# Rotary key by tokens, rotary queries from two half blocks, seven PSUM banks in the first FFN and wider mixer margins in a Hymba-style layer

## The reference

```
h = h + 0.5 * swiglu(rmsnorm(h, g_ffn1), w_gate, w_up, w_down)      # D_FF = 2816
u = rmsnorm(h, g_mix); proj = u @ w_in                              # 1184 columns
c_q (256) | c_kv (128) + k_pe (32) | q_s (512) | k_s (128) | v_s (128) = split(proj)
# latent attention, 8 heads, causal over the whole sequence
q = rmsnorm(c_q) @ w_q_b  -> per head 64 plain + 32 rotary
k_pe = rope(k_pe, cos, sin)                                         # one rotary key for all heads
kv = rmsnorm(c_kv) @ w_kv_b -> per head 64 key + 64 value
s = (q_nope . k_nope + q_pe . k_pe) * 96**-0.5; o_mla = softmax(s) @ v
# local attention, 8 query heads, 2 key heads, window 128, sinks, T5 bias -> o_swa
h = h + concat(rmsnorm(o_mla), rmsnorm(o_swa)) @ w_o
h = h + 0.5 * swiglu(rmsnorm(h, g_ffn2), ...)
out = rmsnorm(h, g_final)

def rope(x, cos, sin):            # x1, x2: the two halves of the last axis (16 + 16)
    return concatenate([x1 * cos - x2 * sin, x2 * cos + x1 * sin])
```

## Time and profile before

| | |
|---|---|
| median of 3 runs | 4984.26 us (4982.69 to 4986.34) |
| profiled execution | 4978.47 us |
| its span (core 2, the slowest) | 4976.9 us |
| spans of the 8 cores | 4958.9 to 4976.9 us |
| TensorE busy | 97% of the span |
| VectorE, ScalarE busy | 56%, 38% |
| GpSimd busy | 2% |

### The profile page before, as it was taken

How to read it: one execution, slowest core, us unless ns; L and a number is a source line. 1 busy time by engine, 2 the same in 40 slices (tenths; PEclk the granted TensorE clock), 3 DMA queues, 4 the chain that set the end, 5 groups by cost and what they waited for, 6 DMA issues and landing times.

```text
span 4976.9 us, 93066 instructions; the slowest of 8 cores (4958.9 to 4976.9 us)
## 1 busy us (share of the span) xinstructions
PE 4827.9 (97%) x29209; PEld 2350.5 (47%) x29784; DVE 2795.0 (56%) x6313; ACT 1895.0 (38%) x3567; POOL 91.2 (2%) x154
## 2 busy tenths in 40 slices
PE   7899999999999999999999999999999999999998
PEld 3344444445444444544544444454544444445444
DVE  4366565555665565564557555555555655555654
ACT  1124425335233342534524243352642423336541
POOL 1100000000000000000000000000000000000000
PEclk9999999999999999999999999999999999999999
DMA  9985754544445454444445445444444545443434
GB/s 180 191 211 123 191 171 124 171 136 147 143 142 178 141 163 149 151 142 131 154 143 178 144 134 174 137 155 147 133 152 141 174 146 177 136 144 110 128 108 143
DMA packets 259288, 751.85 MB, mean 151 GB/s; under 512 B 28320, under 2 KB 36640, under 8 KB 258464
## 3 DMA queue, kind: packets, MB, share of 16 engines
q1 hardware_dynamic: 229664, 648.78, 41.9%
q0 software_dynamic: 28864, 97.07, 8.5%
q10 hardware_dynamic: 288, 0.03, 0.0%
...
## 4 chain that ended last, share of the span: by engine, by line
PE 92%; DMA 4%; DVE 2%; issue 2%; ACT 0%; SPq 0%; DVEq 0%; ACTq 0%; POOLq 0%; POOL 0%
PE ps L565 46%; PE ps L597 23%; PE ps L732 5%; PE ps L886 5%; PE ps L1039 4%; PE ps L906 3%; DMA sb_h<-xT 1%; PE ps L939 1%; PE ps L824 1%; DVE sb_u L533 1%; PE ps L435 1%; PE ps L448 1%; DMA sb_slotB<-wd 1%; PE ps L570 1%; PE ps L965 1%
## 5 line engine op out<-in xcount | busy, mean ns | idle before, releaser
L565 PE MATMUL ps<-sb_u,sb_slotA 128*128 128x512 bf16 x10390 | 2569.7, 380 | 33.4 <-DMA sb_slotA<-wgu 4.1
L565 PEld LDWEIGHTS ps<-sb_u,sb_slotA 128*128 128x128 bf16 x10688 | 999.1, 98 | 1077.2 <-issue 34.5
L597 PE MATMUL ps<-sb_act,sb_slotB 128*128 128x512 bf16 x5473 | 1311.0, 380 | 16.6 <-DMA sb_slotB<-wd 4.7
L584 DVE SCALAR_TENSOR_TENSOR sb_tb<-sb_tb,ps 128x512 f32<-128x512 f32 x704 | 483.0, 686 | 722.8 <-PE ps L565 322.6
L580 ACT ACTIVATE sb_tb<-ps 128x512 f32<-128x512 f32 x704 | 419.6, 596 | 1151.3 <-PE ps L565 927.5
L891 ACT ACTIVATE sb_PT<-ps 128x512 bf16<-128x512 f32 (+3 forms) x1280 | 653.4, 533 | 506.1 <-PE ps L886 364.0
L597 PEld LDWEIGHTS ps<-sb_act,sb_slotB 128*128 128x128 bf16 x5632 | 536.2, 98 | 608.4 <-issue 17.1
L587 DVE TENSOR_TENSOR sb_act<-sb_tb,ps 128x512 bf16<-128x512 f32 x704 | 482.7, 686 | 251.1 <-PE ps L565 212.5
L604 DVE SCALAR_TENSOR_TENSOR sb_h<-ps,sb_h 128x512 f32<-128x512 f32 x544 | 375.0, 690 | 409.2 <-PE ps L597 347.7
L886 PE MATMUL ps<-sb_QT,sb_KT 128*128 128x512 bf16 (+3 forms) x1225 | 407.1, 346 | 1.9 <-ACT sb_PT L891 0.7
L906 PEld LDWEIGHTS ps<-sb_VA,sb_PT 128*128 128x128 bf16 x4352 | 253.5, 98 | 193.4
...
## 6 DMA issues: line engine op xcount, KB each, us to landing
sb_slotA<-wgu2s SPq DMA_DIRECT2D x340, 512.0 KB, 3.5
sb_slotA<-wgu1s SPq DMA_DIRECT2D x308, 512.0 KB, 3.7
...
sb_slotB<-wd2s SPq DMA_DIRECT2D x120, 384.0 KB, 3.2
...
sb_slotB<-wd2s SPq DMA_DIRECT2D x124, 320.0 KB, 2.9
...
```

What stands on the lines that cost most here:

```text
L565: inst = nc.tensor.matmul(PS[bank][:], lhsT=w[:, a, kc, :], rhs=ub[:, kc, :], start=(kc == 0), stop=(kc == 7))
L584: G.op("dve", [("tb", t), P(gb)], [("tb", t)], lambda: nc.vector.scalar_tensor_tensor(out=tb[:, t, :], in0=tb[:, t, :], scalar=1.0, in1=PS ...
L597: inst = nc.tensor.matmul(PS[bank][:], lhsT=w[:, c, :], rhs=act1[:, a0 + c, :], start=(c == 0), stop=(c == nch - 1))
```

## The change

- The rotary key leaves block 3. Its 32 columns are appended to the 128 columns of the local values, so each of the 32 value matmuls has 160 columns, in two banks (two token blocks in each). VectorE rotates the key with the tokens on the partitions by small multiplications with a new table `ropek` (a 128 KB load per tile) and additions into `kttok`, which is cleared at the start of the mixer; TensorE transposes it (4 transposes of 128 columns), ScalarE copies it to head 0 and VectorE to head 1, and two copies give it to heads 2 to 7.
- The rotary queries are made from two blocks, one with the first halves of all 8 heads and one with the second, so two banks of two matmuls in place of four. Products and sums are formed twice as before; four copies of 32 rows x 1024 with a repeated source put each half into place for two heads at a time.
- `fbank` hands out seven banks (ps0 to ps6) in the two-tile FFN, except in its last group.
- The mixer windows end 28 us ahead of the second FFN, 45 us for tile 0 and 30 us for tile 1; the windows of tiles 14 and 15 stay.
- Weight blocks 3, 5 and 11 are loaded with the columns that they have (640, 640, 512 in place of 1024).

```diff
+M_COLS = {3: 640, 5: 640, 11: 512}
+MARG = {0: 45.0, 1: 30.0}
...
+        ropek = sb("ropek", [128, 2, 4, 2, 16], F32, at=aR + 4096)
+        kx = sb("kx", [128, 2, 4, 2, 16], F32, at=aR + 5120)
+        kt_tok = sb("kttok", [128, 4, 128], BF16, at=aR + 6144)
...
+        f_wide = [3]
+
         def fbank():
-            b = f_bank[0] % 3
+            b = f_bank[0] % f_wide[0]
...
+                f_wide[0] = 7 if len(tiles) > 1 and grp is not groups[-1] else 3
...
-            bp = proj(3, True)
-            bq = [proj(0), proj(1)]
+            G.dma("sp", "ropek", [("pace", 0, 0, 16)] if n == 0 else [], [R[2]],
+                  ropek[:].rearrange("p a j x i -> p (a j x i)"), ropek_in[ti], 131072)
+            G.op("dve", [], [R[3]], lambda: nc.vector.memset(kt_tok[:], 0.0), 0.3)
+            bq = [proj(0, True), proj(1)]
             bkv = proj(2)
-            for r0, a in ((64, 0), (96, 1)):
-                G.op("dve", [P(bp), R[0], R[1]], [("KT", ti, 0, 1)], lambda r0=r0, a=a: nc.vector.tensor_tensor(
-                    out=KT[r0:r0 + 32, ti, 0, :], in0=PS[bp][r0:r0 + 32, :], in1=rope[r0:r0 + 32, a, :],
-                    op=ALU.mult), d_dve(512))
-            for lo, hi in ((1, 2), (2, 4), (4, 8)):
...
-            view, mk = m_item(5)
-            wv = view.rearrange("p (k f) -> p k f", k=8)
-            bv = mbank()
+            bv = [mbank(), mbank()]
+            for half, i in enumerate((3, 5)):
+                view, mk = m_item(i)
+                wv = view.rearrange("p (k f) -> p k f", f=160)
+                for j in range(4):
+                    def vmm(j=j, half=half, wv=wv):
+                        inst = None
+                        for k in range(4):
+                            kc = 4 * half + k
+                            inst = nc.tensor.matmul(PS[bv[j // 2]][:, (j % 2) * 160:(j % 2) * 160 + 160],
+                                                    lhsT=um[:, kc, j * 128:(j + 1) * 128], rhs=wv[:, k, :],
+                                                    start=(kc == 0 and j % 2 == 0), stop=(kc == 7),
+                                                    skip_group_check=True)
+                        return inst
+                    G.op("pe", UMK[4 * half:4 * half + 4] + mk, [P(bv[j // 2])], vmm, 4 * 0.07)
+            for x in range(2):
...
+                kp = pv3[:, :, 128:160].rearrange("p j (x i) -> p j x i", x=2)
+                G.op("dve", [R[2]], [("kx", 0), P(b)], lambda kp=kp, o=o: nc.vector.tensor_tensor(
+                    out=kx[:, 0, o:o + 2], in0=kp, in1=ropek[:, 0, o:o + 2], op=ALU.mult), 0.2)
+                for y in range(2):
+                    G.op("dve", [P(b), R[2]], [("kx", 1)], lambda kp=kp, o=o, y=y: nc.vector.tensor_tensor(
+                        out=kx[:, 1, o:o + 2, y, :], in0=kp[:, :, 1 - y, :], in1=ropek[:, 1, o:o + 2, y, :],
+                        op=ALU.mult), 0.18)
+                for par in range(2):
...
+                    G.op("dve", [("kx", 0), ("kx", 1)], [R[3]], lambda ov=ov, o=o: nc.vector.tensor_tensor(
+                        out=ov, in0=kx[:, 0, o:o + 2], in1=kx[:, 1, o:o + 2], op=ALU.add), 0.2)
+            bt = mbank()
+            ktp = PS[bt][:].bitcast(BF16)
...
+                for j in range(4):
+                    inst = nc.tensor.transpose(ktp[:, j * 128:(j + 1) * 128], kt_tok[:, j, :], ident[:])
                 return inst
...
+            G.op("pe", [R[3], ("ident",)], [P(bt)], ktr, 4 * 0.06)
+            G.op("act", [P(bt)], [("KT", ti, 0, 1)], lambda: nc.scalar.copy(
+                out=KT[64:128, ti, 0, :], in_=ktp[64:128, 0:512]), d_act(512))
+            G.op("dve", [P(bt)], [("KT", ti, 1, 1)], lambda: nc.vector.tensor_copy(
+                out=KT[64:128, ti, 1, :], in_=ktp[0:64, 0:512]), d_dve(512))
...
-            for qd in range(2):
-                ba, bb = qmm(qs1, qd), qmm(qs1, 2 + qd)
...
+            ba, bb = qmm(qs1, 0), qmm(qs1, 1)
+            for x, (p1, p2, op) in enumerate(((ba, bb, ALU.subtract), (bb, ba, ALU.add))):
...
+                for pr in range(4):
+
+                    G.op("dve", [("Z", 3)], [("Y", 2 * pr, 1 + x), ("Y", 2 * pr + 1, 1 + x)],
+                         lambda pr=pr, x=x: nc.vector.tensor_copy(
+                             out=QT[64 + 32 * x:96 + 32 * x, 2 * pr:2 * pr + 2, :],
+                             in_=qr[32 * pr:32 * pr + 32, :].unsqueeze(1).to_broadcast([32, 2, T])), d_dve(1024, 4))
...
-                win[n] = (max(prev, phase_at[(0, n, "e")]), phase_at[(1, n, "s")] - 14.0)
+                win[n] = (max(prev, phase_at[(0, n, "e")]), phase_at[(1, n, "s")] - MARG.get(n, 28.0))
```

More of the change, by code:

```diff
@@ L794, in vmm, with ktr @@
+            bt = mbank()
+            ktp = PS[bt][:].bitcast(BF16)
+            def ktr():
                 inst = None
[L795 to L801 removed]
@@ L1028, in mixer @@
                     swa_finish(j // 2)
-            UOK = [("Y", c, x) for c in range(8) for x in range(2)]
+            UOK = [("Y", c, x) for c in range(8) for x in range(3)]
             for dc in range(8):
```

111 lines of the change are left out of this document (56 added, 55 removed).

## The result

The changed kernel took 4910.5 us (median of 4908.5, 4910.5 and 4911.2) against 4985.1 us before (4 runs), ratio 0.985 with a 95% interval of 0.983 to 0.987: faster by 75 us, where 61 were forecast (4923 us, range 4893 to 4952). The profiled executions took 4978.5 and 4910.5 us, 68.0 us apart. In many executions of either kernel the cores of a die ran at a lower granted clock over long stretches (0.80 to 0.82 where a trace shows it); such dies are left out here, and the experiments are compared by the **mean span of the four cores of a die**, over all dies left, beside before on the same chip (standard error about 1 us each). By that measure the change is worth 74.0 us (e12).

What follows compares the result with a forecast made beforehand. TensorE, busy 97%, was taken to bound the kernel. 31.1 + 14 + 13 + 6 - 3 = 61 us off a median of 4984.3 us gave 4923 us, range 4893 to 4952.

Steps and rivals of the forecast that it cites:

- Part 1: Mixer matmuls on TensorE: 12 fewer of 512 columns, wider value matmuls and transposes added; 31.1 us saved over 16 mixers.
- A clock between the two levels: Rival: all cores run between the two clock levels, saved columns worth 16/13, 7 us more in part 1; 4916 us, chance 0.01.
- Part 2: VectorE and ScalarE work in the mixers: the key's new dependence ahead of the transposes costs TensorE 3 us, ends 0 and 16.
- the rotary key stops TensorE: Rival: in every mixer TensorE waits at the four transposes for VectorE's chain, 107 us in all; 5027 us, slower, chance 0.03.
- Part 3: Seven banks in the two-tile FFN at the start: fewer waits for VectorE's bank reads, 14 us back, ends 3 and 28.
- only some 8% of room: Stretches from 50 to 250 us: the DMA queue has only 8% of room, 15 us in 200, if weights are needed earlier.
- Part 4: Larger margins ahead of second FFNs: 13 us back at the middle tiles, 6 at tile 1, 0 at tile 0.
- tile 1's boundary: Second FFN of tile 1, margin grown to 30 us: 6 us back, ends 0 and 11.
- tile 0: Tile 0's margin of 45 us: no sign could be fixed, put at 0 with 8 us either way.
- The last two mixers keep their windows: 0: Last two mixers, their windows unchanged: no gain or loss, 0 with 4 us either way.

Runs made afterwards that it cites:

- e12: The changed kernel itself run once more beside the kernel before on the same chip: 4898.3 against 4972.3 us, -74.0 us.
- e7: The changed kernel with 16 extra VectorE multiplications ahead of the rotary key's second half in every mixer: 5013.4 us against 4973.4 us for the kernel before.
- e6: The changed kernel with four extra VectorE multiplications ahead of the rotary key's second half in every mixer: 4910.5 us against 4973.4 us for the kernel before.
- e1: The kernel before with seven PSUM banks for the first FFN as the only edit: 4948.8 against 4971.4 us, -22.6 us.
- e11: The changed kernel with five banks for the first FFN in place of seven: 4902.1 us against 4974.9 us for the kernel before.
- e10: The changed kernel with tile 0's margin at 28 us in place of 45: 4904.4 us against 4974.9 us before, 3.5 us worse than the changed kernel.

## Why the prediction was right, and where its steps were not

**Part 1** had 31.1 us; 28.9 came on core 2 and 30.6 as the mean of the eight cores. (The bound named beside it, a loss of 50 us if a wide matmul cost 0.216 us, is 44 when worked out again: 2.59 - 5.12 - 0.22 = -2.75 us in each of 16 mixers. Nothing rests on it.) The 160-column matmul was taken at 0.069 us; sixteen of them take 1.27 us with a last one of 0.23, which is 1.04 / 15 = 0.069:

```profile
697.10 1.27 PE L804 MATMUL ps<-sb_slotM,sb_um 128*128 128x160 bf16 x16
```

A clock between the two levels is not what the compared runs had: the granted clock is 0.993, and eight matmuls of 512 columns still take 1.89 us. By the Trainium skill's rule (TensorE: Matmul & The Clock Gate, Part 1) it would be 13/16 for as long as all cores are busy; the traces of the compared cores do not agree.

**Part 2** had 3 us for the key. TensorE waited for `kttok` once, 2.1 us. The last addition ended 1.1 to 2.9 us ahead of the transposes in 14 of 16 mixers, where the forecast had 2 us to spare. The rows for its prices:

```profile
L882 DVE COPY sb_QT<-sb_qr 32x1024 bf16<-32x1024 bf16 x128 | 53.7, 420 | 4.9
L831 DVE TENSOR_TENSOR sb_kttok<-sb_kx 128x64 bf16<-128x64 f32 x64 | 14.4, 224 | 5.7 <-DVE sb_kttok L831 0.2
...
L754 DVE MEMSET sb_kttok<- 128x512 bf16 x16 | 7.8, 485 | 0.9
...
L844 DVE COPY sb_KT<-ps 64x512 bf16<-64x512 bf16 x16 | 6.7, 418 | 22.6 <-PE ps L839 22.6
```

424 was taken for the first (420 came), 0.19 to 0.22 us for the small ones (191 to 224 ns), 430 for the clearing (485), 692 for the copy out of PSUM (418). By the Trainium skill's rule (VectorE: DVE Perf Modes, What auto-detection actually checks) the first is a copy that can run in the fastest mode; the trace agrees, with 420 ns where the slow rate would have given 1.2 us. The rival "the rotary key stops TensorE" priced 16 waits of 5 us with the clock's 1.7 us at 107 us and said slower than before; e7 made much the same case, 15 waits of 4.7 us on average, and lost 103 us against e6. It did not happen in the change because some 2 us of lead were left, and no more than that: four multiplications used it up.

**Part 3** had 14 us with an end of 28; 20.1 came on core 2, 21.5 as the mean of the eight and 22.6 in e1. The reason given for holding back, DMA's share of 0.96 to 1.00, was right in kind and came later than assumed: up to 200 us the share simply rose to 1.02 to 1.06 and the weights were in time, and what remains is the wait for slotB at 214 us. The step that failed is "only some 8% of room". The 5 banks of e11 fit neighbours sharing a bank as the cause.

**Part 4** was right in the middle and wrong at both ends. For the middle tiles it had 13 us; 11.1 came, and the gates' waits there fell from 13.7 to 7.4 us:

```profile
PEld ps L745 <- issue: 9.7, 13, 6.3
PEld ps L579 <- issue: 7.4, 24, 0.6
```

The loss of clock at tiles 3, 7 and 11 is gone (1.00 in the stretch from 1275 us). For tile 1's boundary it had 6 us: the boundary itself gave 2.4 (12.0 to 9.6), and the longer wait for the mixer's weights, which landed in 8.3 us and not in 4.6, took more than that back, so that the stretch lost 5.3. The prediction had no term for that wait. For tile 0 it had 0; 7.4 and 2.2 us came around it on core 2 (3.6 and 3.0 as the mean of the eight), of which e10 puts 3.5 on the margin, with an error of 2. "The last two mixers keep their windows: 0" was the **wrong step**. Their windows are kept, but the order inside them is not. The mixer edit alone loses 19 us there, and tile 13's margin brings it back. That the sum came out right is luck in this point: the two errors are of opposite sign and in different parts. The mixer edit was worth 17 us alone and not 31, and tile 13's margin, which the prediction gave no term, as much more in the changed kernel.

On core 2 the sum was 7 us short between the profiled executions (68 against 61): 6 more at the banks, 7 and 2 around tile 0, 1 at the start, 3 at the end and 3 for the key, less 2 of column work, 2 in the middle and 11 at tile 1.
